# Turning round the column order of the split products' moving operand and output

## The reference

```python
def reference(x, meta_tokens, ...):
    x = first_block(x, meta_tokens, rel_bias, ln_pre_mix, ..., w_in, ..., w_out, w_gate_up, w_down)
    return second_block(x, c_2, positions_2, w_ada_2, ..., w_in_2, ..., w_uq_2, w_ukv_2, w_c_out_2, w_o_2, ...)

# in the first block
proj = jnp.einsum('bld,dc->blc', hn, w_in[layer])
gu = jnp.einsum('bld,df->blf', hn, w_gate_up[layer])
ff = jnp.einsum('blf,fd->bld', jax.nn.silu(gu[..., :D_FF]) * gu[..., D_FF:], w_down[layer])
# in each of the two layers of the second
proj = jnp.einsum("bsd,dp->bsp", u, w_in)
y_c = jnp.einsum("bsc,cd->bsd", o * jax.nn.silu(c_gate), w_c_out)
out = jnp.einsum("bsd,de->bse", m, w_o)
```

## Time and profile before

| | |
|---|---|
| median of 3 runs | 1712.26 us (1709.57 to 1713.22) |
| profiled execution, from its first to its last instruction | 1708.3 us; its time with what lies around the span is not recorded apart |
| TensorE busy | 1687.0 us, 8588 matmuls |
| TensorE weight loads busy | 1401.2 us, beside the matmuls |
| VectorE, ScalarE, GpSimd busy | 1065.2, 723.3 and 154.8 us |
| granted TensorE clock, mean | 0.994 |
| read from and written to the chip's main memory | 171.28 and 4.78 MB |

### The profile page before, as it was taken

One profiled execution on the slowest core, in us unless ns is written; L12 is line 12 of the kernel. 1 busy time (PEld: TensorE's weight loads), 2 busy tenths in 40 slices (PEclk: granted clock), 3 DMA queues, 4 the chain that ended last, 5 costly groups with the idle time before them and its releaser, 6 DMA issues.

```text
span 1708.3 us, 21445 instructions
## 1 busy us (share of the span) xinstructions
PE 1687.0 (99%) x8588; PEld 1401.2 (82%) x8588; DVE 1065.2 (62%) x1779; ACT 723.3 (42%) x1155; POOL 154.8 (9%) x144
## 2 busy tenths in 40 slices
PE   8999999999999999999999999999999999999997
PEld 8877777888888888888888888889888888888886
DVE  7355557766665347745769665657554769667565
ACT  5436664322222237476423222535566533332533
POOL 2100000000000000111100000011211100000012
PEclk9999999999999999999999999999999999999998
DMA  4331012555554321221222222221322122222221
GB/s 178 116 112 50 26 50 87 201 196 194 197 197 160 111 99 75 99 84 65 75 99 92 97 90 94 96 99 50 124 99 75 49 99 99 97 91 90 93 99 50
DMA packets 31138, 177.49 MB, mean 104 GB/s; under 512 B 3677, under 2 KB 5869, under 8 KB 13886
## 3 DMA queue, kind: packets, MB, share of 16 engines
q1 hardware_dynamic: 22048, 144.71, 23.6%
q0 software_dynamic: 8608, 31.21, 5.3%
q10 hardware_dynamic: 382, 0.19, 0.0%
HBM read 171.28 MB, written 4.78 MB: 103 GB/s over the span
## 4 chain that ended last, share of the span: by engine, by line
PE 96%; DVE 2%; DMA 1%; ACT 1%; issue 0%; ACTq 0%; DVEq 0%
PE ps L640 29%; PE ps L642 29%; PE ps L641 28%; PE ps L1264 1%; PE ps L1252 1%; PE ps L875 1%; PE ps L905 1%; PE ps L838 1%; DVE h L1905 1%; PE ps L1099 1%; PE ps L897 1%; PE ps L678 1%; PE ps L870 0%; PE ps L836 0%; DMA w_raw<-in_w 0%; PE ps L849 0%
## 5 line engine op out<-in xcount | busy, mean ns | idle before, releaser
L640 PE MATMUL ps<-Xh,w_hi 128*128 128x512 f32 (+2 forms) x1760 | 667.0, 379 | 4.7 <-DVE y L1905 2.1
L642 PE MATMUL ps<-Xh,w_lo 128*128 128x512 f32 (+2 forms) x1760 | 655.7, 373 | 0.0
L641 PE MATMUL ps<-Xl,w_hi 128*128 128x512 f32 (+2 forms) x1760 | 655.6, 373 | 0.0
L1905 DVE TENSOR_TENSOR w_lo<-w_raw,w_hi 128x2048 fp32r<-128x2048 f32 (+1 forms) x161 | 312.2, 1940 | 252.1 <-ACT w_hi L1344 251.8
L640 PEld LDWEIGHTS ps<-Xh,w_hi 128*128 128x128 f32 x1760 | 331.8, 189 | 68.9 <-issue 10.8
L1344 ACT ACTIVATE w_hi<-w_raw 128x2048 fp32r<-128x2048 f32 (+1 forms) x158 | 260.5, 1652 | 294.1 <-DMA w_raw<-in_w 271.2
L641 PEld LDWEIGHTS ps<-Xl,w_hi 128*128 128x128 f32 x1760 | 332.0, 189 | 59.1 <-issue 2.6
L642 PEld LDWEIGHTS ps<-Xh,w_lo 128*128 128x128 f32 x1760 | 331.6, 188 | 57.9
L1912 DVE SCALAR_TENSOR_TENSOR cacc<-ain,vec,cacc 128x512 f32<-128x512 f32 x240 | 166.4, 764 | 0.0
L1344 ACT ACTIVATE gt<-ps 128x512 f32<-128x512 f32 x48 | 28.6, 596 | 200.7 <-PE ps L642 200.6
L640 PE MATMUL ps<-act_h,w_hi 128*128 128x512 f32 (+1 forms) x192 | 71.5, 373 | 1.7 <-DVE act_l L1905 1.7
(11 more groups left out here) (322 smaller groups left out, 2165.1 us busy)
## 6 DMA issues: line engine op xcount, KB each, us to landing
w_raw<-in_w SPq DMA_DIRECT2D x134, 1024.0 KB, 4.8
ada_w<-in_w_ada POOLq DMA_DIRECT2D x48, 512.0 KB, 4.7
bias_scratch<-brow POOLq DMA_DIRECT2D x2, 1312.0 KB, 6.6
h<-in_xT SPq DMA_DIRECT2D x4, 512.0 KB, 5.9
out<-h SPq DMA_DIRECT2D x8, 256.0 KB, 2.1
bias<-bias_scratch POOLq DMA_DIRECT2D x1, 1024.0 KB, 9.3
bias<-bias_scratch POOLq DMA_DIRECT2D x1, 512.0 KB, 7.4
cact<-in_c POOLq DMA_DIRECT2D x1, 512.0 KB, 6.5
```

Of the source, the lines that this page charges most:

```text
L640: nc.tensor.matmul(o_, whi, xhi, start=start, stop=False)
L641: nc.tensor.matmul(o_, whi, xlo, start=False, stop=False)
L642: return nc.tensor.matmul(o_, wlo, xhi, start=False, stop=stop)
L1905: return nc.vector.tensor_tensor(o_, a_, b_, op)
```

## The change

In `mm3` the output and both moving operands are taken with a step of minus one along their columns. Column 511 (or the last of the slice) is read first and written first, column 0 last. The stationary operands are unchanged, every product computes the same sums into the same places, and no instruction, wait or transfer is added or removed.

```diff
             def mm3(o_, whi, wlo, xhi, xlo, start, stop):
+                o_, xhi, xlo = o_[:, ::-1], xhi[:, ::-1], xlo[:, ::-1]
                 nc.tensor.matmul(o_, whi, xhi, start=start, stop=False)
                 nc.tensor.matmul(o_, whi, xlo, start=False, stop=False)
                 return nc.tensor.matmul(o_, wlo, xhi, start=False, stop=stop)
```

## The result

The changed kernel took 1743.07 us in the median of 4 runs (1740.87 to 1744.59), the kernel before 1710.91 us on the same chips: a ratio of 1.0194, 95% interval 1.0177 to 1.0212. It is slower by 32 us where 24 were forecast.

What follows compares the result with a forecast made beforehand. TensorE, busy 1687.0 of 1708.3 us, was taken to bound the kernel; 3.8 ns on each of 6240 split products gave 24 us, so 1712.3 + 24 = 1736 us. The range was 1655 to 1762 us, leaving out the half rate.

Steps and rivals of the forecast that it cites:

- The bound and the currency: TensorE, busy 1687.0 of 1708.3 us, bounds the kernel; a split product's start-to-start step, 226.2 ns, reaches the end time.
- The sign: The turned `mm3` products make the kernel slower, by 24 us; chance 0.34, or 0.52 with half rate included.
- The kind: In `mm3`, the loss comes from a changed relation between moving read and weights' read, 3.8 ns a product.
- The step that carried the forecast: In `mm3`, equal offsets of moving tiles and weights were the favoured relation, lost when turned: 226.2 to 230 ns.
- the term 3.8 ns x 6240: 6240 `mm3` products at the cheap step, 5520 wide and 720 of 256 columns, each 3.8 ns dearer: 24 us.
- The nearest row: Ten products from 739.92 to 742.22 us, after the second block's attention scores, 230 ns each, taken as the turned price.
- 456 dear ones: Wide products with `Xh1` moving, value projections, `fox` and `Kh`, already at mixed relations: no change expected.
- The split by width: In `mm3`, 256-column products rise by the same few ns as 512-column ones, the extra belonging to the weight load.
- The story of two reads that cross: In `mm3`, moving read and next product's weight load hinder each other in one memory, 12 ns a product.
- The faster rival: Turned `mm3` reads run one way with the weight load and meet less: 38 us less, 1674 us; chance 0.30.
- The half rate: Falling columns in `mm3` not taken two at a time, at read or PSUM write: 1324 us more, 3036 us; chance 0.18.
- the upper bound: If two columns still go through together, `mm3` products cost at most 235 ns: 8.8 ns x 6240, 55 us more.

Runs made afterwards that it cites:

- the run with the read alone: Only the moving operands of `mm3` read from the last column, output written rising, against the kernel before: 1743.24 us, ratio 1.0196.
- the groups: Output and moving operands in column groups taken last to first, rising inside, against the kernel before: groups of 4, 16, 32, 64 gave 1.0196, 1.0198, 1.0177, 0.9996.

## Why the prediction was right, and where it was off

**The bound and the currency: right.** It was TensorE's start-to-start distance that had to be priced, and the loss came through almost one for one: 32.8 us in wide split products, 33.2 us in the span, with the cover of the other engines untouched.

**The sign: right. The kind: right as far as it was tested.** The step that carried the forecast was that the relation of moving read and weights was the favoured one and would not be kept. The two rising runs with an offset show that this relation sets the price of rising products (64 bytes alone cost 1.9%), the run with the read alone that the read is what the change disturbs, and the groups that order within 256 bytes, the modulus of `in_phase`, is what decides. What is not shown is that the falling read pays for that same relation: at 233.3 ns it did not answer to an offset of 64 bytes or to half the load, and a price of the falling order itself would look the same.

The run with 64 bytes also bears on the rule that the prediction weighed. The Trainium skill, "SBUF — State Buffer", section "Who interferes with whom", has TensorE's two read ports as independent and TensorE waiting on no one. This case doesn't bear that out: weights that lie 64 bytes further on, with every split product otherwise unchanged, made the kernel 1.9% slower.

**The size: the term 3.8 ns x 6240 was mis-sized, twice.** The nearest row, 230 ns, was taken for the price turned round; measured is 233.3 ns. That row is itself a mean of unsettled steps of 224 to 236 ns, and no row before shows 233.3 as a settled price, so that the two lie only 3 ns apart is luck. The price before was read too low as well: 442 steps of 226.2 ns were made of 443 records, but records of 389 ns that start every 226.7 ns can straddle an edge of the window in twos; the starts give 226.7. The step rose by 6.7 ns where it was cheap, not by 3.8, and over all wide products, pauses included, by 5.5 ns x 5976. And 720 narrow products and 456 dear ones were put in the wrong class. The narrow ones became 1.3 ns cheaper at the full clock, and their sum moved by 0.4 us and not 2.7. The dear ones, named as among mixed relations before and after, went to the same 233.3 ns as all others: around 90 us, where the steps were 226 to 237 ns, nearly all starts in the changed trace are 233 or 234 ns apart. The errors partly cancel, 24 against 33 us.

**The split by width: wrong both ways.** The prediction had the extra tied to the weight load, so that narrow products would rise by the same few ns as wide ones; its alternative, a cost per column, had them rise by half as many. They didn't rise; from start to start they fell by 1.3 ns. With an offset of 64 bytes they fell by 4 ns while the wide ones rose. An extra that is rounded to steps of 6.67 ns could do that, if it were rounded differently at the two widths; it was not tested for the narrow ones, and turned round their steps do not settle (mostly 115 to 123 ns).

**The story of two reads that cross: half fallen.** The prediction had them disturb each other for as long as the load lasts. Turned round, half the load and an eighth of it cost the same as the whole; rising, half the load cost 3 ns more. And a falling read of 512 columns takes 233.3 ns at an offset of 0, at one of 64 bytes, with 128, 64 and 16 stationary columns: it answered to nothing of what moved the rising read. The faster rival rested on the two reads meeting less often when both run one way; whichever way the load takes its columns, turning the moving read made the settled step dearer, 226.7 to 233.3 ns. The half rate is ruled out by the same window: 233 ns, not 430. Whether two columns go through together at all, on which the upper bound was conditioned, no run shows.

**What stays open.** Why a falling read settles at 35 units of 6.67 ns and a rising one at equal offsets at 34, and whether the stationary read has any part in the first. Nor is it known why an offset of 128 bytes, or half the load, leaves the rising steps unsettled. A stationary operand read the other way wasn't tried, nor were offsets other than 0, 64 and 128 bytes. The offset of 64 bytes for the narrow products alone was not tried either; by the 4.2 ns of the rising run it should give back about 3 us over 720 products, an estimate.

## What to carry to other kernels

Where TensorE is busy from end to end, read the distance from start to start and compare stretches that differ in where their operands lie: here 1.9% hung on 64 bytes modulo 256 between weights and moving tiles, and an instruction count shows nothing of it. With equal offsets, read moving operands of 512 columns rising, or at least rising within 256 bytes; the direction of the output was free. And before a cost is put down to a resource, halve the use of that resource: here it took one pair of runs to see that the cost does not shrink with the size of the weight load.

## What was not expected of the hardware

The steps of the split products, where they are stable, are all multiples of 6.67 ns: 113.3 and 120 ns at 256 columns, 226.7 and 233.3 at 512, and 504 columns settle at the same 226.7 ns as 512. Where they are not stable, their means are no such multiples (229.8, 232.4 ns). A falling write into PSUM costs nothing (ratio 0.9998). The falling read of this kernel does not answer to 64 bytes of offset between weights and moving tiles (1743.07 and 1744.16 us), and the rising one does (about 1710 and 1741.6 us). And the offset that costs 512-column products 6.7 ns a step gives 256-column products 4 ns (119.7 to 115.5 ns).
